# A norm folded into the projection behind it, and position tables made earlier and skewed at loading

## The chip, the cores and the metric

The kernel runs on one core of a Trainium2 chip. The metric is the time of one execution on the device in microseconds, the median of several.

## The reference, cut to what matters

512 tokens of 1024 channels pass two blocks one after the other. The first (an LRU mixer, a sparse-attention mixer, each followed by a convolutional FFN) ends with a norm. The second begins each of its two layers with a norm of its own and four mixers, one of which adds a bias that depends on the distance of two tokens.

```python
def rms_norm(x, g):
    xf = x.astype(jnp.float32)
    y = xf * lax.rsqrt(jnp.mean(xf * xf, axis=-1, keepdims=True) + EPS)
    return (y * g.astype(jnp.float32)).astype(x.dtype)
...
    return rmsnorm(h, final_norm_g)        # end of the first block
...
    for i in range(DEPTH):                 # second block
        h = rms_norm(x, g_mix[i])
        ... = jnp.split(h @ w_in[i], offsets, axis=-1)
        ...
        bias = jnp.transpose(rel_bias[t5_bucket(kpos[None, :] - qpos[:, None])], (2, 0, 1))
        ...
        x = x + merged @ w_out[i]
```

So the residual of the second block is the normed output of the first, and layer 0 takes a norm of a norm. Both can be written over the raw sum x: with r1 = rsqrt(mean(x²)+eps) and the gain g1 of the final norm, the second norm is x · (g1·g) · rsqrt(mean((x·g1)²) + eps·(mean(x²)+eps)).

## The kernel before

The residual XT lies in SBUF as 8 tiles of 128 channels by 512 tokens. The program is a row of stages; each `stage` ends with all engines meeting. SP issues the loads (weights go through RING, a ring of slots), PE multiplies, ACT and DVE split each float into a rounded high part and a low rest, so that a product is three matmuls (`three`, L394 to L396).

A projection starts before its norm is known ("DEFER"). In `mix_project(l)` DVE and ACT make XH = XT · gain and XL; ACT then squares XT into eight tiles (L338), DVE adds these up in six additions (`defer_sums`, L359), and PE, in its own order, does the first two units (`first_units`, L449 to L464), waits for the sixth addition, multiplies by ones (`defer_pe`, L370 and L371), and only then takes the third unit (`project(2)`). DVE turns the sum into a mean (L377), ACT takes the root, DVE the reciprocal R = wk(9), and DVE multiplies every unit by R as it takes it from PSUM. The order on each engine is the order written in the code.

Between `ffn(1)` and `mix_project(0)` lies a stage that the change removes (L2590 on). In it PE looks up the bias rows (L2607) from a one-hot table HOT, DVE copies them, SP writes 16 KB to memory (`bias_rows`) and reads them back as shifted windows of 128 partitions (BIAS, 1792 KB), PE reverses the order of the partitions with a matmul by `flip` (L2615), DVE negates them (L2629), and SP stores 1792 KB (`bias_tables`). Beside this, ACT, PE and DVE norm XT in place with `final1_g` (L284, L293, L299, L303, L306). The stage `grouped(l)` loads `bias_tables` in each layer, and `differential(l)` behind it uses them.

Two more stages are touched. In the compression stage of the sparse attention DVE fills BLK (L1242), PE multiplies it with the weights nsa_w1 (L1265) for v = 0 and v = 1, and ACT evicts. In `out_stage`, the output projection of a layer, eight units of 24 matmuls follow each other, for each of which DVE makes two low parts (L391), and at the end DVE adds the eight banks to XT (L553).

Of the kernel before, what the change touches and what calls it, by code (L numbers as in the profile page):

```python
# [14 lines left out]
P = 128  # L15
TOK = 512
TT = TOK // P
D = 1024
# [52 lines left out]
def const_tables():  # L71
# [4 lines left out]
        "flip": eye[::-1],  # L76
# [96 lines left out]
def build(nc, io):  # L173
# [22 lines left out]
    SM = sbuf("SM", [P, 512])  # L196
    PS = whole.enter_context(nc.psum_tensor("PS", [P, 8, TOK], F32))
# [123 lines left out]
    def defer_act(act, s, gain, at, highs, first, second):  # L321

        first()
        for k in range(BY_DVE, KD):
            nc.scalar.activation(r(highs[k]), XT[:, k], ACT.Copy, scale=par(gain, at + k)).then_inc(s["x_high_act"], 1)
        second()
# [8 lines left out]
    def squares_act(squares):  # L335

        for k in range(KD):
            yield nc.scalar.activation(squares[k], XT[:, k], ACT.Square)  # L338
# [6 lines left out]
    def defer_dve(dve, s, gain, at, highs, lows, first, second):  # L345

        for k in range(BY_DVE):
            nc.vector.tensor_scalar(r(highs[k]), XT[:, k], par(gain, at + k), None, ALU.mult).then_inc(s["x_high"], 1)
        first()
        for k in range(KD):  # L350
            if k == KD // 2:
                second()
            high_ready(dve, s, k)
            nc.vector.scalar_tensor_tensor(out=r(lows[k]), in0=XT[:, k], scalar=par(gain, at + k),
                                           in1=r(highs[k]).bitcast(F32), op0=ALU.mult, op1=ALU.subtract).then_inc(s["x_low"], 1)

    def defer_sums(dve, s, squares):

        add = lambda a, b: nc.vector.tensor_tensor(squares[a], squares[a], squares[b], ALU.add).then_inc(s["paired"], 1)  # L359
        for k in (0, 2, 4, 6):  # L360
            dve.wait_ge(s["squared"], k + 2)
            add(k, k + 1)
        dve.wait_ge(s["paired"], 4)
# [9 lines left out]
    def defer_inverse(dve, s, before, between):  # L373
# [3 lines left out]
        nc.vector.tensor_scalar(wk(8), bank(7), 1.0 / D, EPS, ALU.mult, ALU.add).then_inc(s["mean"], 1)  # L377
# [90 lines left out]
    def out_stage(w, src, following):  # L468
# [4 lines left out]
        with stage("used x_first highs lows banked added") as (block, s):  # L473
# [65 lines left out]
            def _(dve):  # L539
# [10 lines left out]
                every_unit(dve, unit)  # L550
# [331 lines left out]
    def ffn(l, following):  # L882
# [6 lines left out]
        with stage("used a_scaled conv gelu gated dve_step padded" + DEFER) as (block, s):  # L889
# [27 lines left out]
            def _(act):  # L917
                high = lambda u, j, i: weight_high(act, s, w, u, j, i, WH, s["used"])
                defer_act(act, s, "ffn_g", l * KD, XH, lambda: high(0, 0, 0), lambda: high(1, 1, 0))
# [24 lines left out]
            def _(dve):  # L944
# [3 lines left out]
                defer_dve(dve, s, "ffn_g", l * KD, XH, XL, lambda: low(0, 0), lambda: low(1, 1))  # L948
# [166 lines left out]
    with stage("in_proj free v_feat v_turned g_w g_high g_low g_in g_feat g_turned w2 v_out gates gates_seen" + DEFER) as (block, s):  # L1115
# [45 lines left out]
        def _(act):  # L1161
# [4 lines left out]
            defer_act(act, s, "nsa_g", 0, XH, lambda: high(0), lambda: high(1))  # L1166
# [19 lines left out]
        def _(dve):  # L1186
# [4 lines left out]
            defer_dve(dve, s, "nsa_g", 0, XH, XL, lambda: low(0), lambda: low(1))  # L1191
# [24 lines left out]

    ROWS = KV * N_CMP
# [5 lines left out]
    with stage("used blocks hidden turned act_in padded k_in v_in k_out v_out") as (block, s):  # L1223
        @block.sync
        def _(sp):
            prefetch(sp, nsa_w1)
            prefetch(sp, nsa_out)
            stream(sp, nsa_w1, s["used"])

        @block.vector  # L1230
        def _(dve):
            for v in range(2):
                for h in range(2):
                    for q in range(2):
                        rows = slice(64 * q, 64 * q + 64)
                        for a in range(2):
                            for odd in range(2):
# [5 lines left out]
                                                        src[:, odd, :, a:a + N_CMP], pos, ALU.add).then_inc(s["blocks"], 1)  # L1243
            nc.vector.memset(HID, 0.0).then_inc(s["padded"], 1)
# [13 lines left out]
        def _(pe):  # L1258
            for v in range(2):
# [29 lines left out]
        def _(act):  # L1289
            act.wait_ge(s["padded"], 1)  # L1290
# [18 lines left out]
    with stage("scored maxed exped weighed turned copied summed_v biased o_copied dve_step") as (block, s):  # L1309
# [7 lines left out]
        def counted(n):  # L1317

            return 2 * (n + 1) - (n + STEP) // STEP if n >= 0 else 0

# [176 lines left out]
    rows_dram = nc.dram_tensor("bias_rows", (4, 2 * TOK), F32, kind="Internal").ap()  # L1497
    bias_dram = nc.dram_tensor("bias_tables", (P, 7 * TOK), F32, kind="Internal").ap()
# [34 lines left out]
    def mix_project(l):  # L1533
# [5 lines left out]
        SQ, R, VAR = [ar(8 + k) for k in range(KD)], wk(9), wk(8)  # L1539
        WH = [RING[:, 7, 0:D], wk(10, 2), RING[:, 4, 0:D]]  # L1540
# [14 lines left out]
                "lam_ready dve_step")  # L1555
        with stage(sems + DEFER) as (block, s):
# [10 lines left out]
            def _(pe):  # L1567
# [44 lines left out]
                pe.wait_ge(s["lam_in"], 1)  # L1612
                nc.tensor.matmul(bank(6, 0, 2), cst("ones")[0:DIFF_D], LAM[0:DIFF_D, 0:2], start=True, stop=True).then_inc(s["lam_sum"], 1)
# [71 lines left out]
            def _(act):  # L1685
# [29 lines left out]
                defer_act(act, s, "mix_g", l * KD, XH, lambda: high(0), lambda: high(1))  # L1715
# [7 lines left out]
                defer_root(act, s)  # L1723
                nc.scalar.preload_act_table(ACT.Silu)
# [54 lines left out]
            def _(dve):  # L1779
# [39 lines left out]
                defer_dve(dve, s, "mix_g", l * KD, XH, XL, lambda: low(0), lambda: low(1))  # L1819
                defer_sums(dve, s, SQ)  # L1820

# [9 lines left out]
                defer_inverse(dve, s, third, next_two)  # L1831
# [103 lines left out]
                low(21)  # L1935
                for c in range(2):
# [5 lines left out]
    def grouped(l):  # L1942
        with stage("bias o_out" + ATT) as (block, s):
# [13 lines left out]
            def _(sp):  # L1957
                sp.dma_start(ar(7, 7), bias_dram).then_inc(s["bias"], 16)
# [852 lines left out]
```

## Time and profile before

| | |
|---|---|
| runs | 3823.07 us median of 3 (3822.71 to 3826.91) |
| the profiled execution | 3824.66 us, its span 3822.9 us |
| granted TensorE clock, mean | 0.96 |
| busy: PE, DVE, ACT, POOL | 94%, 45%, 30%, 1% of the span |

The span runs from the first to the last instruction; the time of the execution is 1.8 us more. Busy shares are means over some forty stages with different limits, so what an edit is worth is read in its own stage. The granted clock is in parts of 2.4 GHz: 1.00 is that level, 0.50 is 1.2 GHz.

### The profile page before, as it was taken

The page shows a single profiled execution, that of the slowest core. Times are in us where ns is not written, and L with a number is a line of the kernel's source. Part 1 is how long each engine was busy: PE and PEld are TensorE (multiplying, and loading weights), DVE is VectorE, ACT ScalarE, POOL GpSimd, SP SyncE. Part 2 cuts the span into 40 slices and gives each one's busy share as a digit, 9 for nine tenths or more (in the row PEclk, how much of TensorE's full clock was granted, in tenths as well). Part 3 has the DMA queues.
Part 4 walks back from the last instruction along what each step waited for, and adds up shares of the span by engine and source line. Part 5 has one row for each costly group of instructions (what it writes and reads, how often), then busy time and mean ns, then how long its engine had stood idle before and what let it go on. Part 6 is the DMA issues. An engine that isn't in the chain of part 4 may idle for free. (4 is left out here: it accounts for less than half of the span.)

```text
span 3822.9 us, 44287 instructions
## 1 busy us (share of the span) xinstructions
PE 3577.9 (94%) x16700; PEld 2371.1 (62%) x16700; DVE 1728.3 (45%) x2838; ACT 1139.0 (30%) x1782; POOL 41.6 (1%) x20
## 2 busy tenths in 40 slices
PE   8899999889999998988998999999988997999997
PEld 6778877755788766646875333437735875434335
DVE  6565535478555438475333111137566334011116
ACT  5632223157322223354321000013355332000003
POOL 0000000021000000000000000000000000000000
PEclk9999999999999999988998999999989998999999
DMA  4223232200233222102216999971211223999981
GB/s 153 91 91 96 88 100 98 85 10 2 100 98 98 89 76 83 66 20 73 96 67 247 397 419 408 407 301 56 63 46 46 96 95 158 377 409 408 415 371 55
DMA packets 109592, 616.66 MB, mean 161 GB/s; under 512 B 12524, under 2 KB 13044, under 8 KB 59672
## 3 DMA queue, kind: packets, MB, share of 16 engines
q1 hardware_dynamic: 109464, 614.94, 42.4%
q8 instruction: 82, 1.34, 0.1%
q14 instruction: 46, 0.38, 0.0%
HBM read 610.94 MB, written 3.95 MB: 161 GB/s over the span
## 5 line engine op out<-in xcount | busy, mean ns | idle before, releaser
L396 PE MATMUL PS<-WK_r,RING_r 128*128 128x512 f32 x1920 | 748.8, 390 | 0.0
L394 PE MATMUL PS<-WK_r 128*128 128x512 f32 x1448 | 565.1, 390 | 0.0
L396 PEld LDWEIGHTS PS<-WK_r,RING_r 128*128 128x128 f32 x1920 | 359.9, 187 | 77.4
L388 ACT ACTIVATE WK_r<-RING 128x1024 fp32r<-128x1024 f32 x212 | 223.4, 1054 | 451.7 <-PE PS L396 369.8
L2489 DVE TENSOR_TENSOR XT<-XT,PS 128x512 f32<-128x512 f32 x128 | 88.0, 688 | 580.9 <-PE PS L2402 580.9
L395 PE MATMUL PS<-HT_r,WK_r 128*128 128x512 f32 (+1 forms) x896 | 348.6, 389 | 0.0
L391 DVE TENSOR_TENSOR RING_r<-RING,WK_r 128x1024 fp32r<-128x1024 f32 x212 | 259.0, 1222 | 185.5 <-ACT WK_r L388 185.5
L394 PEld LDWEIGHTS PS<-WK_r 128*128 128x128 f32 x1448 | 271.3, 187 | 57.5 <-issue 0.5
L395 PE MATMUL PS<-HT_r,RING_r 128*128 128x512 f32 (+1 forms) x752 | 296.4, 394 | 0.0
L394 PE MATMUL PS<-AR_r,RING_r 128*128 128x512 f32 x640 | 251.2, 392 | 25.1 <-DVE HT_r L391 25.1
L396 PE MATMUL PS<-AR_r,RING_r 128*128 128x512 f32 x672 | 263.1, 391 | 0.0
L391 DVE TENSOR_TENSOR RING_r<-RING,RING_r 128x1280 fp32r<-128x1280 f32 (+2 forms) x96 | 132.4, 1381 | 276.5 <-ACT RING_r L388 276.5
L395 PE MATMUL PS<-AR_r,WK_r 128*128 128x512 f32 (+1 forms) x552 | 214.7, 389 | 0.0
L388 ACT ACTIVATE RING_r<-RING 128x1280 fp32r<-128x1280 f32 (+2 forms) x96 | 113.7, 1185 | 308.1 <-PE PS L396 269.2
L395 PEld LDWEIGHTS PS<-HT_r,WK_r 128*128 128x128 f32 (+1 forms) x896 | 167.7, 187 | 35.4 <-issue 0.5
L2390 PE MATMUL PS<-AR,HT 128*64 128x512 f32 x768 | 184.4, 613 | 2.2 <-ACT HT L2462 2.2
L2390 PE MATMUL PS<-AR,RING 128*64 128x512 f32 x768 | 180.7, 601 | 0.0
L2390 PE MATMUL PS<-AR,WK 128*64 128x512 f32 x768 | 170.0, 599 | 6.2 <-ACT WK L2469 6.2
L2378 PEld LDWEIGHTS PS<-WK 128*128 128x128 f32 x1024 | 126.8, 198 | 70.9 <-issue 70.9
L395 PEld LDWEIGHTS PS<-HT_r,RING_r 128*128 128x128 f32 (+1 forms) x752 | 141.8, 189 | 32.1 <-issue 1.0
L391 DVE TENSOR_TENSOR AR_r<-AR,WK_r 128x512 fp32r<-128x512 f32 (+1 forms) x74 | 51.2, 692 | 244.1 <-ACT WK_r L388 243.9
L394 PEld LDWEIGHTS PS<-AR_r,RING_r 128*128 128x128 f32 x640 | 121.3, 190 | 52.8 <-DVE RING_r L391 27.5
(425 smaller groups left out, 5172.8 us busy)
## 6 DMA issues: line engine op xcount, KB each, us to landing
AR<-moe SPq DMA_DIRECT2D x288, 1024.0 KB, 9.8
RING<-moe SPq DMA_DIRECT2D x96, 1024.0 KB, 10.7
RING<-ff_in SPq DMA_DIRECT2D x96, 512.0 KB, 3.5
RING<-branch SPq DMA_DIRECT2D x64, 640.0 KB, 3.9
RING<-ff_out SPq DMA_DIRECT2D x48, 512.0 KB, 3.5
RING<-mix_in SPq DMA_DIRECT2D x44, 512.0 KB, 3.5
RING<-ple SPq DMA_DIRECT2D x16, 640.0 KB, 12.9
RING<-nsa_in SPq DMA_DIRECT2D x16, 512.0 KB, 3.5
```

The source lines that it names most:

```text
L388: return nc.scalar.activation(r(out), x, ACT.Copy)
L391: return nc.vector.tensor_tensor(r(out), x, r(high).bitcast(F32), ALU.subtract)
L394: nc.tensor.matmul(out, r(w_high), r(x_high), start=start, stop=False)
L395: nc.tensor.matmul(out, r(w_high), r(x_low), start=False, stop=False)
L396: return nc.tensor.matmul(out, r(w_low), r(x_high), start=False, stop=stop)
L2378: mm = nc.tensor.matmul(bank(k // 4, (k % 4) * P, P), HN[:, t, k * P:(k + 1) * P], HOTS[:, t, bass.ds(i * P, P)], start=(t == 0), stop=(t ...
L2390: mm = nc.tensor.matmul(bank(b + half)[e * CAP:(e + 1) * CAP], rows[:, k, e * CAP:(e + 1) * CAP], w[:, e * D + half * TOK:e * D + (half + ...
L2489: v.tensor_tensor(XT[:, k], XT[:, k], bank(6 + k % 2), ALU.add).then_inc(s["added"], 1)
```

## The change

1. The stage between `ffn(1)` and `mix_project(0)` is gone, and with it the norm in place, the reversal, the negation and `bias_tables`. The `flip` table leaves the constants.
2. `mix_project(0)` takes the raw XT with the gain G12 = mix_g · final1_g. ACT squares twice: XT · final1_g (SQ) and XT (SQ1); DVE adds both sets; PE sums both; DVE makes three instructions of the mean (`both_means`); ACT takes a second root, DVE a second reciprocal R1 later in the stage. One wait is added on PE ahead of the small lam_sum matmul.
3. `out_stage` of layer 0 rescales XT by final1_g · R1 in eight DVE instructions behind unit 4's low parts.
4. The compression stage loads HOT, PE makes the bias rows ahead of its own work, ACT copies them negated, DVE makes G12, and SP writes the 16 KB. The attention stage after it copies the rows 128 times in memory (`bias_spread`, 2 MB). `grouped` of both layers loads the skewed table from it: 128 partitions by 4 runs of 896 elements, each partition one element earlier.

```diff
+    rows_dram = nc.dram_tensor("bias_rows", (4, 2 * TOK), F32, kind="Internal").ap()
+    spread_dram = nc.dram_tensor("bias_spread", (P, 8 * TOK), F32, kind="Internal").ap()
+    everywhere = bass.AP(tensor=rows_dram.tensor, offset=0, ap=[[0, P], [1, 8 * TOK]])
@@ compression stage
             prefetch(sp, nsa_w1)
+            sp.dma_start(HOT, io["hot"]).then_inc(s["hot"], 16)
             prefetch(sp, nsa_out)
             stream(sp, nsa_w1, s["used"])
+            sp.wait_ge(s["rows_out"], 1)
+            sp.dma_start(rows_dram, BIAS_ROWS).then_inc(s["rows_stored"], 16)
+            sp.wait_ge(s["rows_stored"], 16)
...
         def _(pe):
+            pe.wait_ge(s["hot"], 16)
+            for b in range(2):
+                mm = nc.tensor.matmul(bank(3 + 4 * b)[0:4], par("rel_bias", 0, 4)[0:BUCKETS], HOT[:, b * TOK:(b + 1) * TOK],
+                                      start=True, stop=True)
+            mm.then_inc(s["rows"], 1)
...
         def _(act):
+            act.wait_ge(s["rows"], 1)
+            nc.scalar.activation(BIAS_ROWS..., PS[0:4, 3:8:4], ACT.Copy, scale=-1.0).then_inc(s["rows_out"], 1)
@@ attention stage
+        def _(sp):
+            sp.dma_start(spread_dram, everywhere).then_inc(s["spread"], 16)
+            sp.wait_ge(s["spread"], 16)
@@ mix_project, PE
                 for mm in first_units(pe, s, WH, [slot(w, u) for u in range(2)], (0, 1), XH, XL):
                     mm.then_inc(s["in_proj"], 1)
+                if not l:
+                    pe.wait_ge(s["paired1"], 6)
+                    nc.tensor.matmul(bank(6), cst("ones"), SQ1[0], start=True, stop=False)
+                    nc.tensor.matmul(bank(6), cst("ones"), SQ1[4], start=False, stop=True).then_inc(s["summed1"], 1)
                 defer_pe(pe, s, SQ)
                 project(2)
@@ mix_project, ACT
-                for ins in squares_act(SQ):
+                for ins in squares_act(SQ, None if l else column("final1_g", 0)):
                     ins.then_inc(s["squared"], 1)
+                if not l:
+                    for ins in squares_act(SQ1):
+                        ins.then_inc(s["squared1"], 1)
@@ mix_project, DVE
                 defer_sums(dve, s, SQ)
+                if not l:
+                    defer_sums(dve, s, SQ1, "squared1", "paired1")
+                def both_means():
+                    dve.wait_ge(s["summed1"], 1)
+                    step(v.tensor_scalar(R1, bank(6), 1.0 / D, EPS, ALU.mult, ALU.add))
+                    step(v.tensor_scalar(VAR, bank(7), 1.0 / D, None, ALU.mult))
+                    v.scalar_tensor_tensor(out=VAR, in0=R1, scalar=EPS, in1=VAR, op0=ALU.mult, op1=ALU.add).then_inc(s["mean"], 1)
...
                 low(21)
+                if not l:
+                    dve.wait_ge(s["root1"], 1)
+                    step(v.reciprocal(R1, R1))
@@ grouped
-                sp.dma_start(ar(7, 7), bias_dram).then_inc(s["bias"], 16)
+                sp.dma_start(BIAS, skewed).then_inc(s["bias"], 16)
@@ out_stage, DVE
+                        if u == 4:
+                            for k in range(KD):
+                                rescale(k).then_inc(s["scaled"], 1)
```

Three places show the new order. The first is DVE at the sums of squares in `mix_project(0)`; AR holds the squares, WK the means and R, HT_r the low parts XL. Before:

```order
L354 SCALAR_TENSOR_TENSOR HT_r<-XT,PAR,WK_r 128x512 x4
L359 TENSOR_TENSOR AR<-AR 128x512 x6
L391 TENSOR_TENSOR RING_r<-RING,RING_r 128x1024
L391 TENSOR_TENSOR RING_r<-RING,RING_r 128x64
L377 TENSOR_SCALAR WK<-PS 128x512
L391 TENSOR_TENSOR RING_r<-RING,RING_r 128x1024
L391 TENSOR_TENSOR RING_r<-RING,WK_r 128x1024
L380 RECIPROCAL WK<-WK 128x512
```

The same place after the change:

```order
L359 SCALAR_TENSOR_TENSOR HT_r<-XT,SM,WK_r 128x512 x4
L364 TENSOR_TENSOR AR<-AR 128x512 x12
L399 TENSOR_TENSOR RING_r<-RING,RING_r 128x1024
L399 TENSOR_TENSOR RING_r<-RING,RING_r 128x64
L1875 TENSOR_SCALAR R<-PS 128x512
L1876 TENSOR_SCALAR WK<-PS 128x512
L1877 SCALAR_TENSOR_TENSOR WK<-R,WK 128x512
L399 TENSOR_TENSOR RING_r<-RING,RING_r 128x1024
L399 TENSOR_TENSOR RING_r<-RING,WK_r 128x1024
L388 RECIPROCAL WK<-WK 128x512
```

Twelve additions stand where six stood, ahead of the low part of the third unit, and three mean instructions where one stood (R in a row is the new tile R1).

The second place is PE in the same stage, from the end of the first two units to the third. Before:

```order
L464 MATMUL PS<-HT_r,RING_r 128x512 x8
L464 MATMUL PS<-HT_r,WK_r 128x512 x8
L370 MATMUL PS<-AR,CST 128x512
L371 MATMUL PS<-AR,CST 128x512
L394 MATMUL PS<-WK_r,RING_r 128x512
L395 MATMUL PS<-HT_r,RING_r 128x512
```

And after:

```order
L472 MATMUL PS<-HT_r,RING_r 128x512 x8
L472 MATMUL PS<-HT_r,WK_r 128x512 x8
L1640 MATMUL PS<-AR,CST 128x512
L1641 MATMUL PS<-AR,CST 128x512
L375 MATMUL PS<-AR,CST 128x512
L376 MATMUL PS<-AR,CST 128x512
L402 MATMUL PS<-WK_r,RING_r 128x512
L403 MATMUL PS<-HT_r,RING_r 128x512
```

The new pair comes first and waits for the last of DVE's twelve additions; everything behind it on PE waits with it.

The third place is DVE in `out_stage` of layer 0 around unit 4 (each pair of L399 rows is one unit's low parts), after the change:

```order
L399 TENSOR_TENSOR AR_r<-AR,WK_r 128x512
L399 TENSOR_TENSOR RING_r<-RING,WK_r 128x1024
L2654 SCALAR_TENSOR_TENSOR XT<-XT,PAR,R 128x512 x8
L399 TENSOR_TENSOR AR_r<-AR,WK_r 128x512
L399 TENSOR_TENSOR RING_r<-RING,WK_r 128x1024
```

Before, the two pairs stood next to each other; the eight rescalings are now between them.

## Rows read from the trace of the kernel before

**Rows 1.** The head of the page.

```profile
span 3822.9 us, 44287 instructions
```

**Rows 2.** Busy time by engine in the removed stage (window, length, engines, clock, DMA).

```profile
1408.30:1444.34 36.04, 18.88 (x36) 6.67 (x36) 14.90 (x19) 6.18 (x10) 0.00 (x0) 0.78 0.28 107
```

**Rows 3.** Timeline of DVE, end of ffn(1) to the reciprocal of mix_project(0) (idle before in brackets).

```profile
1402.56 5.45 DVE L553 TENSOR_TENSOR XT<-XT,PS 128x512 f32<-128x512 f32 x8 [2.62 <-PE PS L396]
...
1428.57 5.39 DVE L306 SCALAR_TENSOR_TENSOR XT<-XT,PAR,WK 128x512 f32<-128x512 f32 x8
...
1454.42 3.81 DVE L359 TENSOR_TENSOR AR<-AR 128x512 f32<-128x512 f32 x6
1458.14 1.35 DVE L391 TENSOR_TENSOR RING_r<-RING,RING_r 128x1024 fp32r<-128x1024 f32 x2
1460.30 0.69 DVE L377 TENSOR_SCALAR WK<-PS 128x512 f32<-128x512 f32 x1 [0.81 <-PE PS L371]
...
1463.18 3.35 DVE L380 RECIPROCAL WK<-WK 128x512 f32<-128x512 f32 x1
```

**Rows 4.** Timeline of PE, the removed stage and the start of mix_project(0).

```profile
1411.78 3.57 PE L2607 MATMUL PS<-HT,PAR 32*4 32x512 f32 x4 [4.50 <-DMA HT<-hot]
...
1434.55 1.37 PE L2615 MATMUL PS<-AR,CST 128*128 128x448 f32 x2 [4.09 <-DVE WK L2629]
1445.48 3.60 PE L449 MATMUL PS<-WK_r,RING_r 128*128 128x512 f32 x8 [9.56 <-ACT RING_r L388]
...
1456.22 1.98 PE L464 MATMUL PS<-HT_r,WK_r 128*128 128x512 f32 x8
1458.28 1.12 PE L370 MATMUL PS<-AR,CST 128*128 128x512 f32 x2
...
1460.34 0.40 PE L395 MATMUL PS<-HT_r,RING_r 128*128 128x512 f32 x1
```

**Rows 5.** Timeline of ACT: the squares of mix_project(0).

```profile
1448.45 4.26 ACT L338 ACTIVATE AR<-XT 128x512 f32<-128x512 f32 x8
```

**Rows 6.** Windows around three changes of the granted clock (seventh figure from the left).

```profile
1418.00:1418.50 0.50, 0.50 (x3) 0.26 (x2) 0.00 (x0) 0.00 (x0) 0.00 (x0) 0.98 0.00 0
...
1435.00:1436.00 1.00, 0.92 (x2) 0.00 (x0) 1.00 (x3) 0.00 (x0) 0.00 (x0) 0.54 0.00 0
...
1448.50:1449.00 0.50, 0.50 (x3) 0.36 (x3) 0.50 (x2) 0.50 (x3) 0.00 (x0) 0.76 0.00 0
```

**Rows 7.** Timelines of DVE and PE: a gap and a wait inside mix_project(0).

```profile
1477.91 1.22 DVE L391 TENSOR_TENSOR RING_r<-RING,RING_r 128x1024 fp32r<-128x1024 f32 x1 [0.66 <-ACT RING_r L388]
...
1500.11 0.66 PE L1626 MATMUL PS<-CST,WK 8*128 8x8 f32 x8 [0.36 <-DVE WK L1873]
```

**Rows 8.** Timelines of DVE and ACT in out_stage of layer 0, units 4 to 6.

```profile
1991.55 1.22 DVE L391 TENSOR_TENSOR RING_r<-RING,WK_r 128x1024 fp32r<-128x1024 f32 x1
1996.38 0.69 DVE L391 TENSOR_TENSOR AR_r<-AR,WK_r 128x512 fp32r<-128x512 f32 x1 [3.61 <-ACT WK_r L388]
...
2000.20 0.63 ACT L388 ACTIVATE WK_r<-AR 128x512 fp32r<-128x512 f32 x1 [3.86 <-PE PS L396]
```

**Rows 9.** Timelines of SP, DVE and PE in the compression stage.

```profile
744.41 1.76 SPq L256 DMA_DIRECT2D RING<-nsa_w  x4
...
744.46 19.06 DVE L1242 TENSOR_TENSOR WK<-AR,PAR 64x248 f32<-64x248 f32 x32 [0.32 <-PEq L236]
...
753.98 16.76 PE L1265 MATMUL PS<-RING,WK 128*124 128x256 f32 x64 [10.63 <-DVE WK L1242]
```

**Rows 10.** DMA issues of the page: size of one, us from issue to landing.

```profile
AR<-bias_rows SPq DMA_DIRECT2D x1, 1792.0 KB, 6.5
...
HT<-hot SPq DMA_DIRECT2D x1, 128.0 KB, 3.5
```

**Rows 11.** Timelines of SP and ACT: table load and last work of grouped(0).

```profile
1640.59 0.33 SPq L1958 DMA_DIRECT2D AR<-bias_tables  x1
...
1671.68 1.08 ACT L1970 ACTIVATE WK<-PS 128x512 f32<-128x512 f32 x2 [1.20 <-PE PS L1032]
```

More of the change, by code:

```diff
@@ L319, in build, with column, defer_act @@
     BY_DVE = 6
-    def defer_act(act, s, gain, at, highs, first, second):
+    def column(name, at):
+        return lambda k: par(name, at + k)
+    def defer_act(act, s, gain, highs, first, second):
         first()
         for k in range(BY_DVE, KD):
-            nc.scalar.activation(r(highs[k]), XT[:, k], ACT.Copy, scale=par(gain, at + k)).then_inc(s["x_high_act"], 1)
+            nc.scalar.activation(r(highs[k]), XT[:, k], ACT.Copy, scale=gain(k)).then_inc(s["x_high_act"], 1)
         second()
@@ L333, in high_ready, with squares_act @@
             eng.wait_ge(s["x_high_act"], k - BY_DVE + 1)
[L335 removed]
+    def squares_act(squares, gain=None):
         for k in range(KD):
[L338 removed]
+            yield nc.scalar.activation(squares[k], XT[:, k], ACT.Square, scale=gain(k) if gain else 1.0)
     def defer_root(act, s):
@@ L472, in out_stage @@
         trips = w.units // w.slots
-        with stage("used x_first highs lows banked added") as (block, s):
+        with stage("used x_first highs lows banked added scaled") as (block, s):
             def every_unit(eng, body):
@@ L549, in unit @@
                     low_part(slot(w, j), slot(w, j), WH[j % 2]).then_inc(s["lows"], 1)
-                every_unit(dve, unit)
+                if rescale:
+                    for u in range(w.units):
+                        unit(0, u, u)
+                        if u == 4:
+                            for k in range(KD):
+                                rescale(k).then_inc(s["scaled"], 1)
+                    dve.wait_ge(s["scaled"], KD)
+                else:
+                    every_unit(dve, unit)
                 for m in range(KD):
@@ L1222, in build @@
     VC = wk(17, 2).rearrange("p (t c) -> p t c", t=TT)
-    with stage("used blocks hidden turned act_in padded k_in v_in k_out v_out") as (block, s):
+    with stage("used blocks hidden turned act_in padded k_in v_in k_out v_out hot rows rows_out rows_stored gain") as (block, s):
         @block.sync
@@ L1308, in build @@
     NMC, RSC, RCC, COC = NMC[0], RSC[0], RCC[0], COC[0]
-    with stage("scored maxed exped weighed turned copied summed_v biased o_copied dve_step") as (block, s):
+    with stage("scored maxed exped weighed turned copied summed_v biased o_copied dve_step spread") as (block, s):
         halves = [slice(0, 64), slice(64, 128)]
@@ L1539, in mix_project @@
         SQ, R, VAR = [ar(8 + k) for k in range(KD)], wk(9), wk(8)
+        SQ1 = [ar(16 + k) for k in range(6)] + [ar(0), ar(1)]
+        gain = column("mix_g", l * KD) if l else lambda k: G12[:, k:k + 1]
         WH = [RING[:, 7, 0:D], wk(10, 2), RING[:, 4, 0:D]]
```

102 lines of the change are left out of this document (37 added, 65 removed).

## Prediction, made before the changed kernel was run

> **What bounds the kernel now.** I read the busy times first: PE works for 94% of a span of 3822.9 us [rows 1], so almost everywhere the kernel is as long as its matmuls, and an edit on DVE, ACT or SP counts only where PE waits for it. Then I read the windows of the stage that goes. It lasts 36.04 us and PE is busy for 18.9 of them, partly at a low clock (mean 0.78) [rows 2]. The timelines show a chain of one thing after another: PE waits 4.50 us for HOT, and 4.09 us for DVE's evictions [rows 4], and after the last eviction SP still issues a 1792 KB store, until whose end nobody begins the next stage. Nothing of another stage lies beside it, so its whole length is on the path. Last I read the three places where the work goes instead: the start of `mix_project(0)`, the output projection of layer 0, and the compression stage.
>
> **The removed stage.** Minus 36.04 us [rows 2]. The stage in front ends with eight additions from 1402.56 to 1408.01 [rows 3]; the windows cut the removed stage from the first instruction behind them to the first of the mix stage, so one meeting of the engines is in the 36.04 and one remains. The mix stage's weights are prefetched during the output projection of `ffn(1)`, long before, so it finds them without the removed stage's time too. Below I write times in the mix stage as in the trace of before.
>
> **Start of `mix_project(0)`.** Before: DVE's six additions begin at 1454.42 and the next instruction at 1458.14, so six take 3.72 [rows 3]. PE ends its first two units at about 1458.2 and begins the sum of squares at 1458.28; the third unit's second matmul is issued at 1460.34, its first some 0.2 before, so a pair of sums costs about 1.9 [rows 4].
> After: ACT squares twice. The second eight run from 1448.45 + 4.26 = 1452.7 to 1457.0 [rows 5], before DVE wants them. DVE's second six end at 1458.14 + 3.72 = 1461.86. PE's new pair waits for them, so PE stands from 1458.2 to 1461.9 (+3.6) and then does two pairs instead of one (+1.9): the third unit starts 5.5 us later. That is the first cost, **+5.5**.
> DVE's own chain is later by more. Its mean began 2.0 us after L370 started (1460.30 against 1458.28) [rows 3, 4]. Now both sums must be in: 1461.9 + 2.0 + 1.9 = 1465.8, and three instructions of about 0.7 (L377 is 0.69) end at 1467.9 instead of 1460.9: 7.0 later. From there to 1500 DVE works almost without a gap. It takes back 0.66 at 1477.91, where it waited for ACT, which waits for PE, leaving 6.3. At 1500.11 PE already waited 0.36 for DVE's scans [rows 7]. There DVE is 6.3 late and PE 5.5: PE waits another **+0.8**. Behind it both are equally late, and no further wait of PE on DVE shows before the stage ends.
> The second reciprocal (as L380, 3.35 us [rows 3]) stands behind the last weight's low part, where DVE mostly waits for PE and PE wants nothing more of it but evictions. Nothing; without that cover, at most its 3.4.
>
> **The clock.** In the removed stage PE stood idle for 4.09, and right behind the idle time the granted clock went from 1.00 to the lower level of 1.2 GHz (0.54 in the window from 1435) [rows 4, 6]. The new wait of 3.6 us is nearly as long, and so I expect the same. How long it lasts: PE restarted at 1411.78 and had the full clock at 1418.0, 6.2 us later; it restarted at 1445.48 and had it at about 1448.7, 3.2 us later [rows 4, 6]. At half the clock half of that is lost: 1.6 to 3.1. I take **+2.2**, on PE and, where it falls on the sums, on DVE alike. Low bound 0 (the clock stays), high bound 3.4.
>
> **Output projection of layer 0.** DVE's low parts of unit 4 end at 1992.77, those of unit 5 start at 1996.38 and last 1.83 [rows 8]. The eight rescalings have the shape of L306 x8, 5.39 us [rows 3]. They would end at 1998.1, and unit 5's low parts at 1999.9. ACT's next split, which waits for the end of PE's unit 4, starts at 2000.20 [rows 8]; PE needs unit 5 about then. 0.1 to 0.3 us to spare: **0**. PE's matmuls of unit 4 hide it; if the rescalings cost their single durations (8 x 0.74) PE waits 0.3.
>
> **Compression stage.** HOT alone lands in 3.5 us; it is issued after four 512 KB weights, from 744.41 to 746.2 [rows 9, 10]. Low bound 749.7. Behind 2 MB at the rate of the `bias_rows` load (1792 KB in 6.5 us) it is 7.4 us after 744.41: 751.8, which I take. The two lookups took 3.57 us at the low clock [rows 4]: 755.4. PE's own first half began at 753.98, when DVE's first half of BLK was ready [rows 9], so it starts 1.4 late, in a stretch at half clock, of which half is won back since the full clock comes no later. PE's second half waits for DVE's second half, which ends at 744.46 + 19.06 = 763.5 anyway. **+0.6**, from 0 (DVE remains the limit) to 3 (HOT lands with the last weights and delays all). ACT's copy of the rows lies in its long wait; the 16 KB store is issued during v = 1 and hides behind the rest of the stage. If that cover were gone it would cost some 2 us.
>
> **The spread and the skewed load.** The copy of 2 MB in memory has the whole attention stage, eight pairs of heads, behind which no wait stands before its end. At the rate of the shifted load, reading and writing 2 MB each, it is some 15 us: nothing. The skewed load replaces a load that is issued at 1640.59; the stage's last work ends at 1672.76 [rows 11], 32 us of cover. The nearest row is the shifted load of the removed stage, also 512 runs of 896 elements, each a step of one element apart: 6.5 us [rows 10]. So nothing, twice.
> The Trainium skill, "DMA: Bandwidth & Descriptors", section "How a descriptor splits into AXI transactions", speaks against this edit: a descriptor that does not start on a 256-byte boundary also fetches the bytes below its start. By that rule I estimate a run of 3584 bytes at 15 transactions where 14 would do, 7% more on a load that stays hidden; this case's shifted load, whose runs start anywhere too, shows no more than 6.5 us [rows 10].
>
> **The first load.** The constants lose 64 KB at the very start. At the rate above that is 0.2 us at most; **-0.1**.
>
> **Sum.** -36.0 + 5.5 + 0.8 + 2.2 + 0.6 - 0.1 = -27.0 us. The profiled execution took 3824.66, so it would take 3797.7. It is 1.6 above the median of the three runs (3823.07), for which the sum gives 3796.1.
>
> **The rivals.**
> - *The waits cost less.* The clock stays up during the new wait, and HOT is in before BLK. For it: the idle time of 3.6 is shorter than the 4.09 seen. Then -36.0 + 5.5 + 0.8 - 0.1: about 3793. Against it: the length is close to the one that lost the clock. Chance 0.15.
> - *DVE becomes the bound of the mix stage.* It gets about 4 us of additions, 1.3 of means, and a reciprocal. If PE's clock is low during the sums and more of DVE's deadlines than that at 1500 have no slack, the stage gives back 14 rather than 8.5, and HOT costs its 3: about 3804. For it: DVE has only small gaps until 1527. Against it: the one wait of PE on DVE in the stage is 0.36 [rows 7]. Chance 0.08.
> - *No change to speak of.* The removed stage's length would have to be given back by something in the whole. Only a chain of both costs above could do a good part, and none comes near 36. Chance 0.02.
> - *Slower, by the skewed load.* Its source is four bytes out of step from partition to partition. If it took longer than the 32.2 us of cover, `grouped` would end late in both layers; past 32.2 + 27/2 = 45.7 us each, under 41 KB/us, the kernel is slower than before. At 50 us each: 3796 + 2 x 17.8 = 3832. For it: this access pattern on `bias_spread` has no row. Against it: the shifted load reached 276 KB/us. Chance 0.03.
>
> **How the numbers follow.** 0.2% of 3823 is 7.6 us, about what a measurement can tell from no change. My forecast has 0.72, the cheaper case 0.15, the dearer 0.08, no change 0.02, slower 0.03. Faster: 0.72 + 0.15 + 0.08 = 0.95. Predicted time 3796. The range takes the low bounds at one end (-30, 3792, and a run's scatter of some two us below it) and the high ones at the other (clock 3.4, HOT 3, rescaling 0.3: 3800, and as much scatter): 3790 to 3802.
>
> **What would show it.** Right: no stage between the XT additions and the mix stage; PE stands about 3.6 us ahead of the first new sum, named as waiting for DVE's additions; the clock near 0.5 there for 3 to 6 us; PE's wait at the scans grows to about 1.2; in the compression stage a wait on HOT until about 751.8; no wait of PE at unit 5 of the output projection; both skewed loads land in 6 to 9 us. Wrong: a wait on DVE at other units of the mix stage, HOT after 755, PE waiting at unit 5, a load that lands after `grouped`'s last work, or a mix stage whose start is later than the end of the additions by more than the 0.3 us of today's meetings.

## The result, and the profile after

The changed kernel takes 3798.94 us, median of four runs (3797.43 to 3801.82), the kernel before 3823.89 beside it (3822.71 to 3826.91, four runs). The ratio is 0.9931, with a 95% interval of 0.9918 to 0.9943: 24.95 us faster. Forecast were 3796 (3790 to 3802) and a gain of 27.0. The profiled execution is the longest of the four, 3801.82; where [rows 1] has 3822.9, it has:

```profile
span 3800.1 us, 44230 instructions
```

I first cut both traces into stages, each from its first instruction to that of the next. Beside them stand two more profiles of the changed kernel (again, third), taken later. In us:

| stage | before | changed | again | third |
|---|---|---|---|---|
| compression | 33.5 | 38.4 | 36.9 | 37.3 |
| attention | 182.2 | 183.3 | 182.3 | 182.3 |
| output projection behind it | 46.0 | 47.6 | 46.0 | 46.0 |
| removed stage | 36.1 | 0 | 0 | 0 |
| mix stage, layer 0 | 150.6 | 155.1 | 156.3 | 156.3 |
| state-space, layer 0 | 45.7 | 47.3 | 47.7 | 47.7 |
| differential, layer 0 | 70.1 | 70.1 | 68.2 | 68.2 |
| output projection, layer 0 | 47.5 | 47.6 | 48.6 | 48.5 |

The removed stage is gone with its whole length. Two stages are several us longer in every profile: compression and the mix stage. The others differ by 1 to 2 us in one profile and not in the next, although their code is one and the same, so a single profile is no evidence on them. That holds for the kernel before too, of which there is one profile; its mix stage, unchanged in a kernel below that keeps the norm, took 149.3 there.

**The mix stage.** The timeline of PE in the changed kernel, which answers to [rows 4] and the second row of [rows 7]:

```profile
1416.37 2.45 PE L457 MATMUL PS<-WK_r,RING_r 128*128 128x512 f32 x8 [2.14 <-ACT RING_r L396]
...
1426.54 1.97 PE L472 MATMUL PS<-HT_r,WK_r 128*128 128x512 f32 x8
1432.91 2.07 PE L1640 MATMUL PS<-AR,CST 128*128 128x512 f32 x2 [4.39 <-DVE AR L364]
1434.77 1.66 PE L1641 MATMUL PS<-AR,CST 128*128 128x512 f32 x2
1436.27 1.02 PE L375 MATMUL PS<-AR,CST 128*128 128x512 f32 x2
...
1438.22 0.39 PE L403 MATMUL PS<-HT_r,RING_r 128*128 128x512 f32 x1
...
1478.70 0.66 PE L1669 MATMUL PS<-CST,WK 8*128 8x8 f32 x8 [1.08 <-DVE WK L1930]
```

The stage begins at 1415.26 (before: 1444.37). PE stands 4.39 us, named as waiting for DVE's additions. The first pair of sums starts 17.65 us into the stage where the only pair had started after 13.91, 3.7 later. It takes 3.36 us (1432.91 to 1436.27) where a pair at the full clock takes 1.7 (1434.86 to 1436.58 in the run with the third unit first, below). At the scans (L1669) PE waits 1.08 instead of 0.36. The timeline of DVE answers to [rows 3]: twelve additions instead of six, and three instructions of the mean.

```profile
1425.31 7.54 DVE L364 TENSOR_TENSOR AR<-AR 128x512 f32<-128x512 f32 x12
1432.77 1.35 DVE L399 TENSOR_TENSOR RING_r<-RING,RING_r 128x1024 fp32r<-128x1024 f32 x2
1438.19 0.69 DVE L1875 TENSOR_SCALAR R<-PS 128x512 f32<-128x512 f32 x1 [4.07 <-PE PS L376]
...
1442.52 3.35 DVE L388 RECIPROCAL WK<-WK 128x512 f32<-128x512 f32 x1
```

The windows around the sums (seventh figure: granted clock, as in [rows 6]) show the fall to 1.2 GHz while PE stands, and the return 3.4 us later:

```profile
1432.00:1433.00 1.00, 0.09 (x1) 0.09 (x1) 1.00 (x3) 0.65 (x1) 0.00 (x0) 0.82 0.12 49
1433.00:1436.00 3.00, 3.00 (x4) 1.42 (x5) 1.12 (x2) 0.00 (x0) 0.00 (x0) 0.50 0.00 0
1436.00:1437.00 1.00, 1.00 (x3) 0.38 (x2) 0.00 (x0) 0.00 (x0) 0.00 (x0) 0.97 0.00 0
```

**Compression.** The timeline of PE, against the last row of [rows 9]:

```profile
754.46 3.57 PE L1286 MATMUL PS<-AR,PAR 32*4 32x512 f32 x4 [10.29 <-DMA AR<-hot]
757.96 15.14 PE L1295 MATMUL PS<-RING,WK 128*124 128x256 f32 x56
774.11 1.99 PE L1295 MATMUL PS<-RING,WK 128*124 128x256 f32 x8 [1.02 <-DMA RING<-nsa_w]
```

PE waits for HOT until 754.46 and begins its own products at 757.96; seen from the start of the stage that is 3.2 us later than before. At the end a wait of 1.02 for the last weights comes on top. SP's queue shows HOT issued fifth, behind four weights, and the second weights issued 3 us later in the stage than before, since PE frees their slots later:

```profile
745.23 1.76 SPq L257 DMA_DIRECT2D RING<-nsa_w  x4
747.04 0.46 SPq L1247 DMA_DIRECT2D AR<-hot  x1
...
761.76 6.51 SPq L265 DMA_DIRECT2D RING<-nsa_w  x4
768.48 0.32 SPq L1251 DMA_DIRECT2D bias_rows<-AR  x1
```

The full clock comes later too. PE's products run at 1.2 GHz until 14.8 us into the stage before and until 18.4 after. The windows in which the clock rises (stage starts 744.4 and 745.2), first before, then changed:

```profile
759.00:760.00 1.00, 1.00 (x6) 0.82 (x5) 0.94 (x3) 0.00 (x0) 0.00 (x0) 0.88 0.82 262
```

```profile
763.00:764.00 1.00, 1.00 (x5) 0.78 (x4) 0.94 (x3) 0.00 (x0) 0.00 (x0) 0.68 0.54 205
```

**The parts that were to cost nothing.** DVE in the output projection of layer 0, against [rows 8]: the rescalings end at 1975.15, unit 5's low parts at 1976.9, and DVE then waits 2.01 for ACT's next split. No wait of PE stands there.

```profile
1968.63 1.22 DVE L399 TENSOR_TENSOR RING_r<-RING,WK_r 128x1024 fp32r<-128x1024 f32 x1
1969.76 5.39 DVE L2654 SCALAR_TENSOR_TENSOR XT<-XT,PAR,R 128x512 f32<-128x512 f32 x8
...
1978.90 0.69 DVE L399 TENSOR_TENSOR AR_r<-AR,WK_r 128x512 fp32r<-128x512 f32 x1 [2.01 <-ACT WK_r L396]
```

The issues of DMAs (KB of one, us to landing), against [rows 10]: the skewed load and the copy in memory are as quick as they needed to be, HOT is not.

```profile
AR<-bias_spread SPq DMA_DIRECT2D x2, 1792.0 KB, 7.6
...
bias_spread<-bias_rows SPq DMA_DIRECT2D x1, 2048.0 KB, 8.6
...
AR<-hot SPq DMA_DIRECT2D x1, 128.0 KB, 7.4
```

### The profile page after: what moved, and what is told of

Same layout as the page of the kernel before. It is cut to its first block and busy times, and to the rows that moved or that the text cites. A ratio compares the mean times of both kernels' runs of the same rounds, so it can differ in the third digit from the quotient of the medians.

```text
span 3800.1 us, 44230 instructions
## 1 busy us (share of the span) xinstructions
PE 3567.8 (94%) x16672; PEld 2367.3 (62%) x16672; DVE 1727.1 (45%) x2837; ACT 1143.0 (30%) x1783; POOL 41.6 (1%) x20
## 5 line engine op out<-in xcount | busy, mean ns | idle before, releaser
L399 DVE TENSOR_TENSOR RING_r<-RING,WK_r 128x1024 fp32r<-128x1024 f32 x212 | 259.0, 1222 | 184.9 <-ACT WK_r L396 184.9
L399 DVE TENSOR_TENSOR RING_r<-RING,RING_r 128x1280 fp32r<-128x1280 f32 (+2 forms) x96 | 132.4, 1381 | 275.8 <-ACT RING_r L396 275.8
L399 DVE TENSOR_TENSOR AR_r<-AR,WK_r 128x512 fp32r<-128x512 f32 (+1 forms) x74 | 51.2, 693 | 240.1 <-ACT WK_r L396 239.9
```

What stands on the lines that cost most here:

```text
L399: return nc.vector.tensor_tensor(r(out), x, r(high).bitcast(F32), ALU.subtract)
```

## The experiments

Each kernel is the changed one with an edit, five runs each unless said otherwise, beside nine runs of the kernel before (3824.16, 3825.04 and 3824.64 in the three groups).

### The changed kernel again, twice

> The changed kernel once more, as the measure for the runs beside it. If the stage lengths of its first profile belong to the kernel, they come back within 0.3 us: compression 38.4 us (33.5 before the change), attention 183.3 (182.2), output projection behind it 47.6 (46.0), mix stage of layer 0 155.1 (150.6). If the smaller ones of these differences are only periods of low clock that fall differently from execution to execution, attention, the output projection and the state-space stage come back different by one to two us, while compression and the mix stage stay where they were. Time 3799, within 2.

> The changed kernel a third time, as the measure beside the next two. Median within 2 us of 3798.8. In the mix stage of layer 0 the low clock at the sums is there in every execution that waits (3.4 to 7 us of it), while the second period of low clock some 80 to 90 us into the stage comes and goes; that second one is why the stage is 155 in one profile and up to 160 in another.

3798.68 us (3797.28 to 3799.80) and 3799.29 (3798.33 to 3800.30). Both times came as expected, the stages in part. Attention and the output projection behind it are back at the values of before. Compression is still 3.4 to 3.8 longer and the mix stage 5.7 longer, but neither stayed where it was (1.1 to 1.5 shorter and 1.2 longer than in the first profile), and the state-space stage moved by 0.4 only. A second period of low clock 80 to 90 us into the mix stage came in none of these three profiles. What makes 156.3 of 155.1 is the fall at the sums, which lasts 6.8 us instead of 3.4 and brings PE to the scans 1.3 later. PE's wait at the sums is there each time (4.39, 3.40 and 3.38 us), and in the two later profiles the clock is low for almost all of both pairs:

```profile
1429.18 2.07 PE L1640 MATMUL PS<-AR,CST 128*128 128x512 f32 x2 [3.40 <-DVE AR L364]
1431.05 1.91 PE L1641 MATMUL PS<-AR,CST 128*128 128x512 f32 x2
1432.75 1.91 PE L375 MATMUL PS<-AR,CST 128*128 128x512 f32 x2
```

What the mix stage won back lies behind its small matmuls of 2 and 4 columns. In the kernel before the clock was low there, here the window behind the same matmuls in the changed kernel stays at 1.00. First before, then changed:

```profile
1524.00:1531.00 7.00, 7.00 (x19) 5.60 (x20) 3.27 (x5) 1.50 (x2) 0.00 (x0) 0.52 0.00 0
```

```profile
1500.00:1510.00 10.00, 10.00 (x59) 8.57 (x58) 6.79 (x12) 2.90 (x4) 0.00 (x0) 1.00 0.19 58
```

### HOT ahead of the weights, twice

```diff
+            sp.dma_start(HOT, io["hot"]).then_inc(s["hot"], 16)
             prefetch(sp, nsa_w1)
-            sp.dma_start(HOT, io["hot"]).then_inc(s["hot"], 16)
```

> HOT is loaded ahead of the four 512 KB weights instead of behind them. Theory A (the compression stage lost 4.9 us because PE stood 10.29 us for HOT, and made its two lookups of 3.57 us only then): HOT lands at about 3.5 us after the stage's start, the lookups are done before DVE's first half of BLK at about 9.5 us, and the stage is 33.5 to 35 us long again; time 3 to 5 us below the changed kernel. Rival B (the full clock comes late after the idle time whatever stands ahead, and the weights behind HOT now come later): the start of the products moves forward by 3 us but the stage stays above 37; the time is the same within 1 us.

> HOT ahead of the weights once more, since its stage was 4 us shorter and its median the same. Theory A (the gain is real and the run before fell on longer periods of low clock elsewhere): compression stage 33.7 to 34.4 again, median 2 to 5 us under the changed kernel beside it. Rival B (what compression gives back is taken by the clock later on): median within 1 us of the changed kernel, with the compression stage short as before.

3799.32 us (3793.58 to 3803.61) and 3798.75 (3791.07 to 3800.09). The stage is 34.3 and 33.5 us long, as in the kernel before. PE has looked the rows up long before they are wanted, and waits for DVE as it used to:

```profile
747.65 3.00 PE L1286 MATMUL PS<-AR,PAR 32*4 32x512 f32 x4 [3.43 <-DMA AR<-hot]
754.85 8.96 PE L1295 MATMUL PS<-RING,WK 128*124 128x256 f32 x32 [4.19 <-DVE WK L1266]
764.43 7.17 PE L1295 MATMUL PS<-RING,WK 128*124 128x256 f32 x32 [0.62 <-DVE WK L1266]
```

In all four profiles with HOT first (these two and two of the kernels below), PE's products start 9.6 us into the stage, as before; in all eight profiles with HOT behind the weights they start at 12.4 to 13.2. So the order of the loads is the cause of the 3 to 4 us that every one of those eight has: that is shown. The wait of 1.0 for the last weights is not part of it. Two of the eight do not have it, and one profile with HOT first does (the last run below). But the medians hardly move. The ten runs have a mean of 3797.8, the fourteen of the changed kernel 3799.05, and they scatter over 12.5 us where those scatter over 4.5. The profile of the first has two periods of low clock of 7 us each in the mix stage (159.7 us) and a state-space stage of layer 1 of 50.3 instead of 47.9; the second has one of 7 and one of 3.4 (156.3), a state-space stage of 47.8, and took 3794.97. Theory A holds for the stage. By the medians rival B's forecast came both times (0.6 above and 0.5 under the changed kernel beside it). On the sum, 1.3 us in the mean of the runs is less than the 4 of the stage, and it is not settled whether the clock takes the rest regularly.

### The third unit ahead of the sums

```diff
                 if not l:
+                    project(2)
+                defer_pe(pe, s, SQ)
+                if not l:
                     pe.wait_ge(s["paired1"], 6)
...
-                defer_pe(pe, s, SQ)
-                project(2)
@@ DVE
+                if not l:
+                    low(2)
                 defer_sums(dve, s, SQ)
```

> In the mix stage of layer 0 PE takes the third unit before the sums of squares, and DVE makes that unit's low part before its additions, so that PE has work while the twelve additions run. Theory A (PE's wait of 4.39 us and the fall of the clock behind it are the cost): PE waits less than 1 us at the sums, the clock stays at 1.00, and the stage is 5 to 6 us shorter: about 3794. Rival B (DVE's chain bounds the front of the stage: twelve additions, three instructions of the mean, then 60 us almost without a gap): DVE comes only 1 to 2 us earlier to its mean, PE's gain comes back as a wait on DVE at a later unit or at the scans (1.08 us now, then 4 or more), and the stage is 1 to 2 us shorter: 3797 to 3798.

3798.61 us (3797.58 to 3801.12); mix stage 157.0. The wait at the sums is gone and the clock stays up, as theory A has it. Then PE waits for DVE at a later place, the small transposes that need R, and there the clock falls:

```profile
1434.86 1.02 PE L375 MATMUL PS<-AR,CST 128*128 128x512 f32 x2
...
1452.89 0.59 PE L1655 MATMUL PS<-CST,AR 8*128 8x8 f32 x4 [3.46 <-DVE AR L1900]
```

```profile
1435.00:1438.00 3.00, 3.00 (x10) 1.28 (x8) 0.00 (x0) 0.00 (x0) 0.00 (x0) 1.00 0.59 175
1452.00:1459.00 7.00, 6.11 (x18) 5.04 (x19) 6.86 (x11) 2.39 (x3) 0.00 (x0) 0.52 0.03 11
```

Rival B has the mechanism: DVE's chain sets when PE can go on, and this other order hid next to none of the work on it. Its size came out worse than rival B had it: the stage is not 1 to 2 us shorter but 157.0 against 155.1 to 156.3, and PE is at the scans after 63.8 us, between the 63.4 and 64.7 of the changed kernel.

### The second additions on POOL

The six additions of SQ1 are issued by POOL beside DVE's six, and PE takes the sum of SQ first.

> The six additions of the second set of squares are made by POOL beside DVE's six, and PE sums the first set first. If DVE's chain is what holds both PE and the front of the stage (rival B of the run before), this one gains more than that one: DVE is free 3.7 us earlier, the sums start when POOL is through, about 1431 against 1432.9, and the stage is 3 to 5 us shorter: 3794 to 3796. If POOL needs over 1.5 us for an addition of 128x512, or slows DVE beside it, the sums start no earlier than before and nothing is gained, or the kernel is slower by what POOL is late.

3803.91 us (3801.31 to 3804.98), 5 slower. The timelines of POOL, DVE and PE:

```profile
1424.58 11.56 POOL L1607 TENSOR_TENSOR AR<-AR 128x512 f32<-128x512 f32 x6 [503.13 <-ACT AR L343]
1424.40 5.85 DVE L364 TENSOR_TENSOR AR<-AR 128x512 f32<-128x512 f32 x6
1436.19 2.08 PE L1652 MATMUL PS<-AR,CST 128*128 128x512 f32 x2 [3.16 <-POOL AR L1607]
```

One addition takes 1.9 us on POOL in the mean against 0.63 on DVE alone, and DVE's own take 0.98 in the mean beside it. The second branch of the expectation came. The means hide two cases; POOL's shortest, median and longest, in ns:

```profile
L1607 POOL TENSOR_TENSOR AR<-AR x6: 1259/1712/3447, 1424.6 to 1434.9; 128x512 f32<-128x512 f32 x6
```

DVE's first four take 0.67 each, and POOL's first, begun 0.2 us behind the first of them, ends only 1.1 after the fourth. From there the two end in turn: POOL at 1428.02, DVE at 1428.58, POOL at 1429.70, DVE at 1430.25, POOL at 1431.37, so 1.1 us for each of POOL's and 0.55 for each of DVE's. POOL's last two, with nothing of DVE beside them, take 1.26.

By the Trainium skill, "SBUF — State Buffer", section "SBUF: two separate sides", an instruction of DVE with two inputs in SBUF and one of GpSimd (POOL) hold a shared pair of ports one after the other. The ends in turn agree with it, and so does the sum: DVE's six additions take 5.85 us beside POOL's and 3.81 alone [rows 3].

### PE kept busy during the wait

```diff
                 if not l:
+                    for n in range(18):
+                        nc.tensor.matmul(bank(5), r(XH[n % KD][:, 0:P]), r(XL[n % KD]), start=True, stop=True)
                     pe.wait_ge(s["paired1"], 6)
```

> The changed kernel with 18 extra matmuls of 128x512 (their result is never read) while PE waits for the additions at the sums of squares, so that PE stands for under 1 us instead of 3.4 to 4.4. Theory A (the idle time brings the clock down): the clock stays at 1.00 at the sums and the third unit, the wait for DVE's additions is filled but ends at the same time, and the mix stage is 1.5 to 3.5 us shorter. Rival B (the clock falls at this place by its own course, whatever PE does): it is at 0.50 for 3 to 7 us as before and the extra matmuls, slowed, delay the sums: the same or 1 to 2 us slower.

3796.46 us (3793.42 to 3800.09); the mean of the five, 3796.6, is 2.5 under that of the changed kernel's fourteen, and the five scatter over 6.7 us. PE's timeline and the window over it:

```profile
1426.57 4.24 PE L1640 MATMUL PS<-HT_r,WK_r 128*128 128x512 f32 x18
1431.10 1.12 PE L1642 MATMUL PS<-AR,CST 128*128 128x512 f32 x2 [0.29 <-DVE AR L364]
1432.06 1.02 PE L1643 MATMUL PS<-AR,CST 128*128 128x512 f32 x2
```

```profile
1424.00:1438.00 14.00, 13.71 (x54) 9.69 (x53) 11.34 (x18) 7.14 (x12) 0.00 (x0) 1.00 0.21 75
```

Theory A holds for the clock: with useless work in the gap it does not fall. PE is at the scans 61.9 us after the stage's start, against 63.4 in the profile after and 64.7 in the two later ones: the fall costs 1.5 us where it lasts 3.4 and 2.8 where it lasts 7. The stage as a whole was 155.1, as long as in the profile after and 1.2 shorter than in the two later ones, since a period of 3.4 us of low clock came 86 us into it. The 1.5 to 3.5 us that were expected of the stage are not shown.

### Only the tables moved, the norm kept

The norm with final1_g stays a stage of its own, in place; the mix stage and the output projection of layer 0 are those of before.

> Only the tables are moved: the norm with final1_g stays a stage of its own, without HOT, reversal and stores, and the mix stage of layer 0 is that of the kernel before. Squares, eight matmuls by ones (0.95 us each, double at the low clock), mean, root, reciprocal 3.35 and eight products of 0.7 follow one another: 20 to 23 us instead of 36.1. Theory (the fold is worth this stage less what it costs in the mix stage): time 3799 + 21 - 5 to 7 = 3812 to 3815, so the tables alone give 9 to 12 of the 25 us and the fold the rest. Rival (the stage was bound by the table's chain of DMAs, the norm is nearly free in it: 12 us alone): 3805 or less, and the fold is worth only 5.

3810.73 us (3807.75 to 3815.10). The stage took 18.3 us, less than I expected; DVE in it:

```profile
1421.74 0.69 DVE L300 TENSOR_SCALAR WK<-PS 128x512 f32<-128x512 f32 x1 [8.15 <-PE PS L294]
1423.12 3.35 DVE L304 RECIPROCAL WK<-WK 128x512 f32<-128x512 f32 x1 [0.70 <-ACT WK L289]
1426.51 5.39 DVE L307 SCALAR_TENSOR_TENSOR XT<-XT,PAR,WK 128x512 f32<-128x512 f32 x8
```

The tables alone are thus worth 14.3 of the gain (3825.04 to 3810.73; the five runs scatter over 7 us), and the fold 12 more (3810.73 to 3799). Of the 36 us, 18 were the table's chain beyond the norm.

### The second set moved to the differential stage

VAR is mean((x·g1)²) + eps·mean(x²) + eps², and the first two terms are one mean of x²·(g1² + eps). So one set of squares with the gain GE = sqrt(g1² + eps) gives it, and the plain mean is wanted only by the output projection. Here its squares and sums stand in the differential stage, beside eight of its items, and the reciprocal R1 moves from the mix stage to the output projection.

```diff
-                for ins in squares_act(SQ, None if l else column("final1_g", 0)):
+                for ins in squares_act(SQ, None if l else (lambda k: GE[:, k:k + 1])):
...
-                    step(v.tensor_scalar(R1, bank(6), 1.0 / D, EPS, ALU.mult, ALU.add))
-                    step(v.tensor_scalar(VAR, bank(7), 1.0 / D, None, ALU.mult))
-                    v.scalar_tensor_tensor(out=VAR, in0=R1, scalar=EPS, in1=VAR, ...)
+                    v.tensor_scalar(VAR, bank(7), 1.0 / D, EPS * EPS, ALU.mult, ALU.add)
@@ differential, ACT
+                    nc.scalar.activation(SQ1[n - 2], XT[:, n - 2], ACT.Square)
@@ differential, PE
+                    mm = nc.tensor.matmul(bank(7), cst("ones"), SQ1[k], ...)
```

> The second set of squares leaves the mix stage: its mean is only needed there inside eps, so one set made with the gain sqrt(final1_g^2 + eps) gives the same VAR, and the plain squares (for the rescaling in the output projection) are made and summed in the differential stage, one square on ACT and one matmul on PE beside each of eight items. Theory A (the whole price of the fold in the mix stage is the second set: 3.7 us of additions that PE waits for, 1.9 of a second pair of sums, the clock that falls behind the wait): no wait of PE at the sums, mix stage 147 to 150.6 us as in the kernel before (151 to 155 without the clock's chance now 155.1 and 156.3), so 5 to 8 us less; the differential stage stays within 1 us: time 3791 to 3793. Rival B (DVE's and ACT's chain of that stage was the limit anyway, and the squares beside the items lengthen each item of the differential stage, 0.5 us each): mix stage 2 us less, differential 4 more: no gain or a loss.

3801.03 us (3795.10 to 3803.03). Both theories are half right. The mix stage fell to 149.1 us, PE waits for no addition, and at the scans it waits 0.39 as in [rows 7]. The differential stage grew to 75.7. An item there is one chain, and ACT's rows show the square (L2187) between the copy of one item and the exponential of the next:

```profile
1666.26 0.60 ACT L1093 ACTIVATE WK<-PS 128x512 f32<-128x512 f32 x1 [0.54 <-PE PS L1045]
1666.76 0.62 ACT L2187 ACTIVATE RING<-XT 128x512 f32<-128x512 f32 x1
1667.28 0.71 ACT L1085 ACTIVATE WK<-WK,SM 128x512 f32<-128x512 f32 x1
```

### The same with HOT first

> The same and HOT loaded ahead of the weights. If the two costs are independent, compression is 34.3 us again as in the run with HOT first, and the time is 4 us below the one with the second set moved alone: 3787 to 3789. If the clock only moves its low periods elsewhere, as the equal medians of HOT last and HOT first (3798.7 and 3799.3) would allow, the stage is shorter and the time within 1 us of it.

3795.78 us (3794.44 to 3798.14), compression 33.7, mix stage 149.1, differential 75.7. It is 5.3 under the kernel with HOT last in the median and 2.8 in the mean, where 4 were expected; 3787 to 3789 was too low by what the differential stage took.

### The second set in the state-space stage, HOT first

Four squares at the start of the state-space stage of layer 0, four in its end; two additions and six matmuls at its end; ACT takes the root straight from PSUM.

> As the kernel with the second set moved and HOT first, but the squares and their sum are made in the state-space stage of layer 0: four squares on ACT at its start, four in its end, two additions on DVE and six matmuls on PE at its end, where norm, root and reciprocal follow one another and PE stands idle. Theory A (the differential stage lost 6 to 9 us because each of its items is one chain through ACT, and the squares stood in it; the end of the state-space stage has room on ACT and PE): mix stage 149, state-space stage 47.4 to 48.5, differential 66 to 70: 3787 to 3790, the fastest of all. Rival B (there is no such room: the squares at the start delay the first exponential, the matmuls the end): state-space stage 50 or more, 3793 or above.

3789.69 us, four runs (3787.15 to 3789.91), ratio to before 0.9910 (0.9895 to 0.9925): the fastest, 9.6 under the changed kernel beside it. Mix stage 147.4, state-space stage 46.0, differential 68.7, compression 35.4. Theory A. In compression PE waits 1.03 us for the last weights, although HOT is first. The state-space stage has one period of low clock, of 6.8 us, where each profile of the changed kernel has three. The mix stage ran at the full clock throughout, and the added rows of PE and ACT end before DVE's last products, at 1604.3:

```profile
1411.16:1558.54 147.38, 144.03 (x670) 112.12 (x671) 98.06 (x153) 54.91 (x78) 0.00 (x0) 1.00 0.23 67
```

```profile
1597.87 4.45 PE L2071 MATMUL PS<-RING,CST 128*128 128x512 f32 x10
...
1602.37 0.69 ACT L2120 ACTIVATE R<-PS,SM 128x512 f32<-128x512 f32 x1 [2.94 <-PE PS L2071]
```

## Why the prediction was right, point by point

- **The removed stage, -36.0.** Right: 36.06 by the table, and no cover was lost.
- **PE at the sums, +5.5.** Right in both parts. The first pair starts 3.7 later (3.6 forecast). The second pair is there: 1.8 where the clock stays up (1431.10 to 1432.92 in the run with PE kept busy), 1.9 forecast.
- **The clock, +2.2.** Right in kind, and shown by the run with PE kept busy: 1.5 or 2.8, by the execution.
- **The scans, +0.8.** 0.72 (1.08 against 0.36). With the two terms above PE should be 8.5 late there. It was 7.7 in the profile after (63.4 against 55.7) and 8.9 in the two later ones.
- **The length of the mix stage** was not forecast apart from this, and the sum took 8.5 for it. It grew by 4.5 and 5.7 only, since the low clock that the kernel before had behind its small matmuls (6.8 us of it) did not come in these three profiles. That was luck for the forecast: the sum holds no term for it. In the first profile with HOT first, where it came, the stage is 159.7, 9.1 more than before.
- **Compression, +0.6 (0 to 3).** The step that failed. It grew by 3.4 to 6.3 in eight profiles with HOT behind the weights (36.9 to 39.8), on average by 4.7, in each of them by more than the upper bound of 3. Three premises were off. The prediction counted the 7.4 us of 2 MB from the issue of the first weight; they ran from HOT's own issue, 1.8 us later, so HOT landed 9.2 us into the stage instead of 7.4 and PE's products began 3.2 later instead of 1.4. It held that half of that is won back, "since the full clock comes no later"; the full clock came 18.4 us into the stage instead of 14.8, although PE was at its lookups from 9.2 us on, so nothing was won back. And it held that PE's second half waits for DVE anyway. Before, that half began at 763.57, right as PE's first half and DVE's fill (763.52) both ended, so there was no slack to take a late first half. That is the common part, 3 to 4 us. The wait for the last weights (1.02 here, 0 to 1.6 in the others) comes on top; its cause is open. With HOT first the stage is 33.5 to 34.3 in three profiles and 35.4 in a fourth, so with that order the growth is 0 to 1.9, inside the range. The lookup behind PE's own products was not run.
- **The output projection, spread, skewed loads, 0.** Right. The output projection is 1 us longer in the two later profiles (48.5), but just as long in the kernel that keeps the norm and rescales nothing (48.6). Skewed loads took 7.6 us (6 to 9 forecast), under the 32 us of cover, and the straight loads of before 8.1. So the 7% that the prediction estimated from the Trainium skill, "DMA: Bandwidth & Descriptors", section "How a descriptor splits into AXI transactions", do not show here.
- **The first load, -0.1.** Not shown either way. The first stage took 161.0 before and 159.2 to 161.1 in the other profiles.
- **The sum.** -27.0 against -24.95. Compression took 4.1 more than its term and the mix stage 3 to 4 less; the remaining 1 to 2 us are not assigned, and lie within what periods of low clock move between executions. So the nearness of the total rests on two misses that cancel. Two slips in the working changed nothing: the low bound adds up to 3793, not 3792, and the load that would make the kernel slower than before runs at 39 KB/us, not 41.
- **The rivals.** *The waits cost less* is refuted, since the clock fell in each profile that had the wait. *DVE becomes the bound* did not come in the changed kernel, but it was close: with the third unit first PE waited 3.46 us for DVE some 15 us behind the sums. *No change* and *slower* did not come.

## What to carry to other kernels

A load that PE is to wait for is issued ahead of the loads that are only prefetched: 128 KB took 2.3 us in front of four weights and 7.4 behind them. In that stage the late start also moved the return of the full clock, so nothing of the delay was won back there. Work for a value that is needed late is cheapest in a stage that ends in a chain of root and reciprocal, where PE and ACT have nothing to do (46.0 us with it, 45.6 to 50.4 without), and dear in a stage whose items are one chain. Another order on PE gained nothing here while the added work stayed on the engine that PE waits for next.

## What the runs showed of the hardware

- The periods of low clock in the mix stage lasted from 3.4 to 10 us, and they came at other places in another profile of the same program. The lengths of untouched stages therefore take a few values rather than one: state-space 45.6 to 50.4, differential 66.1, 68.2 or 70.1 us. A stage is judged on several profiles. The Trainium skill, "TensorE: Matmul & The Clock Gate", section "What's actually happening", says too that the number of slow matmuls of one kernel varies from run to run. It puts the penalty of the slow start under 1% of a typical kernel. This kernel falls back to the low clock again and again, and its mean granted clock is 0.96; what varies is 4.5 of 3799 us over fourteen runs, while a stage of 46 us varies by 10%.
- A kernel with a shorter stage can scatter more: 12.5 us over ten runs with HOT first, 4.5 over fourteen with HOT last. Why is open.
- Additions of 128x512 on POOL and DVE took turns, 1.1 us for POOL's and 0.55 for DVE's, one ending after the other; POOL's take 1.26 alone, DVE's 0.63.
- In compression the return of the full clock moved with PE's products: 14.8 to 15.0 us into the stage where they began after 9.6 (13.2 in one profile), 17.3 to 18.5 where they began after 12.4 to 13.2.
